# Attention units: the division by the softmax sums moved from VectorE into the turning product on TensorE

## The reference, cut to what matters

```
p = softmax(where(mask, sc, -inf), axis=-1)
attn = p[:, :, 0] - lam * p[:, :, 1]
outs.append(einsum("bhqk,bkhe->bqhe", attn, vb))
```

## Time and profile before

| what | value |
|---|---|
| median of three runs | 2226.13 us (2222.15 to 2226.5) |
| the profiled execution, its own time | 2225.26 us |
| its span, first to last instruction | 2223.5 us |
| its mean granted TensorE clock | 0.908 |
| units of the first attention | about 873 to 905 us |
| units of the two later attentions | about 1530 to 1563 and 1926 to 1960 us |

### The profile page before, as it was taken

The page is one execution under the profiler, slowest core; times in us unless marked ns, Lnnn a source line. Parts: engine busy times, 40 slices in busy tenths (PEclk is TensorE's granted clock), DMA queues, the critical chain, the costliest instruction groups (busy, mean ns, idle before and its releaser), DMA issues.

```text
span 2223.5 us, 33018 instructions
## 1 busy us (share of the span) xinstructions
PE 2064.7 (93%) x13605; PEld 1387.2 (62%) x13605; DVE 717.1 (32%) x2298; ACT 358.4 (16%) x968; POOL 86.6 (4%) x92
## 2 busy tenths in 40 slices
PE   8999999998889798899998989798999999899998
PEld 7687576665655544476665756444688644458863
DVE  4354242221222224532221222457322114732211
ACT  2122110100000012210000100114221001322100
POOL 0112100000000020000000000000001100000110
PEclk9999977998887999977887878899999999999999
DMA  9333359999999973369999999942244344224420
GB/s 344 128 108 115 142 203 398 425 425 424 424 425 425 406 255 113 129 259 426 424 424 424 424 425 423 377 157 76 97 154 155 131 160 165 76 86 152 152 95 19
DMA packets 112382, 565.33 MB, mean 254 GB/s; under 512 B 12456, under 2 KB 15726, under 8 KB 79470
## 3 DMA queue, kind: packets, MB, share of 16 engines
q1 hardware_dynamic: 112238, 563.21, 63.8%
HBM read 562.14 MB, written 1.05 MB: 253 GB/s over the span
## 4 chain that ended last, share of the span: by engine, by line
PE 86%; issue 4%; DVE 4%; DMA 4%; ACT 2%; SPq 1%; DVEq 0%; ACTq 0%
PE ps L2433 14%; PE ps L670 12%; PE ps L1634 11%; PE ps L651 10%; PE ps L296 9%; PE ps L709 7%; PE ps L1201 4%; DMA ring<-in_moe_w_up_dram 3%; PE ps L762 3%; PE ps L1307 3%; PE ps L1211 2%; PE ps L691 2%; PE ps L1975 1%; ACT arena L1771 1%; PE ps L1663 1%
## 5 line engine op out<-in xcount | busy, mean ns | idle before, releaser
L2433 PE MATMUL ps<-arena,ring 128*128 128x256 f32 (+1 forms) x1536 | 305.5, 362 | 0.0
L2433 PEld LDWEIGHTS ps<-arena,ring 128*128 128x128 f32 x1536 | 271.9, 190 | 33.9 <-issue 1.0
L651 PEld LDWEIGHTS ps<-arena 128*128 128x128 f32 x2048 | 251.5, 204 | 28.0 <-issue 27.0
L651 PE MATMUL ps<-arena 128*128 128x32 f32 x2048 | 258.4, 287 | 0.0
L1634 PE MATMUL ps<-ring,arena 128*128 128x512 f32 (+1 forms) x576 | 250.4, 594 | 3.3 <-DVE arena L421 3.3
L670 PE MATMUL ps<-ring,arena 128*32 128x256 f32 x2816 | 195.7, 435 | 41.0 <-issue 38.4
L296 PE MATMUL ps<-ring,arena 128*128 128x512 f32 x480 | 209.1, 596 | 0.8 <-ACT arena L2276 0.8
L1634 PEld LDWEIGHTS ps<-ring,arena 128*128 128x128 f32 x576 | 109.7, 192 | 135.4 <-issue 135.2
L670 PEld LDWEIGHTS ps<-ring,arena 128*32 128x32 f32 x2816 | 114.8, 126 | 121.1 <-issue 86.7
L296 PEld LDWEIGHTS ps<-ring,arena 128*128 128x128 f32 x480 | 91.4, 191 | 113.3 <-issue 111.9
L2493 DVE SCALAR_TENSOR_TENSOR arena<-ps,pcol,arena 128x255 f32<-128x255 f32 (+1 forms) x176 | 84.9, 482 | 210.8 <-ACT arena L2466 207.6
(11 more groups left out here) (305 smaller groups left out, 1904.1 us busy)
## 6 DMA issues: line engine op xcount, KB each, us to landing
ring<-in_moe_w_gate_dram SPq DMA_DIRECT2D x44, 2048.0 KB, 29.3
ring<-in_moe_w_up_dram SPq DMA_DIRECT2D x44, 2048.0 KB, 33.8
ring<-in_moe_w_down_dram SPq DMA_DIRECT2D x44, 2048.0 KB, 29.6
ring<-in_w_up_dram SPq DMA_DIRECT2D x22, 2048.0 KB, 8.0
arena<-in_moe_w_gate_dram SPq DMA_DIRECT2D x20, 2048.0 KB, 30.5
arena<-in_moe_w_up_dram SPq DMA_DIRECT2D x20, 2048.0 KB, 34.9
arena<-in_moe_w_down_dram SPq DMA_DIRECT2D x20, 2048.0 KB, 32.4
ring<-in_ssm_w_in_dram SPq DMA_DIRECT2D x12, 2048.0 KB, 10.2
```

The source lines that it names most:

```text
L651: mm = nc.tensor.matmul(ps[:, 4, k * CAP:(k + 1) * CAP], normed[:, tt, k, :], slots[:, b, tt, :], start=(tt == 0), stop=(tt == TT - 1))
L2433: mm = nc.tensor.matmul(ps[:, n % 4, lo:hi], w[:, k, k4 * P:(k4 + 1) * P], xT_mlp[:, k, lo:hi], start=(k == 0), stop=(k == KD - 1))
```

## The change

The probabilities stay unscaled. DVE writes two diagonal matrices for each unit, the identity times the reciprocal sum of each query row (in the first attention the second also times -lambda), and PE multiplies each 128 x 128 block of exponentials by the diagonal. The product comes out turned and scaled at once. In the first attention the blocks of c = 0 and c = 1 for the same keys are added in PSUM, which replaces `joined`. The diagonals lie in the place of `joined` in the first attention, and in a free area in the later ones. The exps, the mask, the copies out of PSUM and the values are as before. The diff, with the lines left out that only pass a flag on:

```diff
+        diag_first, diag_second = area(14336, 2, 2, P), area(22288, 2, 2, P)
...
         def pe_units(pe, units, pT, probs, joined):
+            inv_diag = diag_first if joined else diag_second
...
                 nk = u.kv // P
-                for c in range(1 if joined is not None else 2):
-                    src = joined[:, b, :] if joined is not None else probs[:, b, c, :]
-                    for kt in range(nk):
-                        at = (c * nk + kt) * P
-                        mm = nc.tensor.transpose(ps[:, 4 + b, at:at + P], src[:, kt * P:(kt + 1) * P], ident)
+                for kt in range(nk):
+                    for c in range(2):
+                        at = kt * P if joined else (c * nk + kt) * P
+                        mm = nc.tensor.matmul(ps[:, 4 + b, at:at + P], probs[:, b, c, kt * P:(kt + 1) * P],
+                                              inv_diag[:, b, c, :], start=(c == 0 or not joined),
+                                              stop=(c == 1 or not joined))
                 mm.then_inc(U["turned"].sem, 1)
...
                 V(nc.vector.reciprocal(st_inv[:, b, :], st_sum[:, b, :]))
-                if joined is not None:
-
-                    if n >= 2:
-                        dve.wait_ge(U["turned"].sem, U["turned"].at(n - 1))
-                    nc.vector.tensor_scalar(st_inv[:, b, 1:2], st_inv[:, b, 1:2], neg_lam, None, ALU.mult)
-                    V(nc.vector.tensor_scalar(joined[:, b, 0:u.kv], probs[:, b, 0, 0:u.kv], st_inv[:, b, 0:1], None,
-                                              ALU.mult))
-                    nc.vector.scalar_tensor_tensor(joined[:, b, 0:u.kv], probs[:, b, 1, 0:u.kv], st_inv[:, b, 1:2],
-                                                   joined[:, b, 0:u.kv], ALU.mult, ALU.add)\
-                        .then_inc(U["probs"].sem, 1)
-                else:
-                    nc.vector.tensor_tensor(probs[:, b, :, 0:u.kv], probs[:, b, :, 0:u.kv],
-                                            bcast(st_inv[:, b, :], u.kv), ALU.mult).then_inc(U["probs"].sem, 1)
+                if n >= 2:
+                    dve.wait_ge(U["turned"].sem, U["turned"].at(n - 1))
+                nc.vector.tensor_scalar(inv_diag[:, b, 0, :], ident, st_inv[:, b, 0:1], None, ALU.mult)
+                nc.vector.tensor_scalar(inv_diag[:, b, 1, :], ident, st_inv[:, b, 1:2], neg_lam if joined else None,
+                                        ALU.mult, *([ALU.mult] if joined else [])).then_inc(U["probs"].sem, 1)
```

More of the change, by code:

```diff
@@ L1740, in values @@
                 nk = u.kv // P
-                if joined is not None:
+                if joined:
                     for kt in range(nk):
@@ L1780, in copy_turned @@
                     act.wait_ge(U["out"].sem, U["out"].at(n - 1))
-                w = u.kv * (1 if joined is not None else 2)
+                w = u.kv * (1 if joined else 2)
                 nc.scalar.activation(pT[:, b, 0:w], ps[:, 4 + b, 0:w], ACT.Copy).then_inc(U["probsT"].sem, 1)
@@ L1855, in hybrid_stack @@
         probs = area(13312, 2, 2, SEQ)
-        joined = area(14336, 2, SEQ)
         pT = area(14848, 2, SEQ)
@@ L1963, in pe_attention1 @@
             pe.wait_ge(jobs_copied.sem, jobs_copied.at(8))
-            pe_units(pe, units, pT, probs, joined)
+            pe_units(pe, units, pT, probs, True)
             pe.wait_ge(U["copied"].sem, U["copied"].at(len(units)))
@@ L2017, in copy_out @@
                                             accum_out=ossq[:, u.i, u.pair:u.pair + 1])
-            act_units(act, units, sm, probs, pT, joined, copy_out)
+            act_units(act, units, sm, probs, pT, True, copy_out)
             head1.act_norm(act)
@@ L2055, in dve_attention1 @@
             dve_jobs(dve, head_jobs)
-            dve_units(dve, units, sm, probs, joined)
+            dve_units(dve, units, sm, probs, True)
             def scale_outputs(half):
@@ L2235, in pe_attention @@
                 pe.wait_ge(jobs_copied.sem, jobs_copied.at(15))
-                pe_units(pe, units, pT2, probs2, None)
+                pe_units(pe, units, pT2, probs2, False)
                 pe.wait_ge(U["copied"].sem, U["copied"].at(n_units))
@@ L2277, in copy_out @@
                                                 ACT.Copy)
-                act_units(act, units, sm2, probs2, pT2, None, copy_out)
+                act_units(act, units, sm2, probs2, pT2, False, copy_out)
                 for tt in range(TT):
@@ L2366, in dve_attention @@
                 dve_jobs(dve, head_jobs, 9)
-                dve_units(dve, units, sm2, probs2, None)
+                dve_units(dve, units, sm2, probs2, False)
                 def normalise(tt):
```

## The result

The changed kernel takes 2231.01 us (median of 11 runs, 2224.13 to 2237.49) against 2223.93 us for the kernel before in the same 11 rounds (2218.17 to 2228.47). The ratio is 1.0031 with a 95% interval of 1.0016 to 1.0045: 0.3% slower, as forecast in direction and in size (0.30%). The interval reaches from 3.6 to 10.0 us around a difference of 7.08. The profiled execution after has a span of 2232.8 us; its own time, 2234.59 us, is 3.6 above the median of its runs.

The account below looks back on a forecast made before the run. A loop of waits through the odd units, with no engine full, was taken to bound the unit stages. First attention 1.4, its lower-clock start 0.8, later attentions 4.6, clock -0.2: +6.6 us, 2232.7 us; range 2227.5 to 2237.5.

Parts of the forecast that it names:

- The forecast pairs: Time from odd turn to odd turn: 3.80 us in the first attention, 4.51 (dilated) and 3.69 (others) in the later ones.
- The price of a product: Turns on PE: a float32 product is two instructions, 0.11 us each further one, so an odd turn takes 1.16 us.
- a product costs four transposes: Rival for the turns on PE: sixteen steps an odd turn, +21 us over the sum, 2253 us; chance 0.03.
- The scaling of the identity: On DVE: costs nothing extra over scaling data, 0.28 us for 128 columns, 0.34 with two column operands.
- The tail of the first stage: End of the first attention: the chain goes from the last scaling to DVE's `scale_outputs`, so the eighth odd turn isn't counted.
- the start of the first attention: First turns at the lower clock, with PE on the chain: 0 to 1.3 us more than counted, taken as 0.8.
- the sum's seven turns and eight scalings: First attention: seven odd turns each 0.72 us longer, eight odd scalings each 0.46 us shorter, together +1.4 us.
- I wrote that it isn't full: PE in the first attention's pairs: busy 3.4 us of 3.80 after the change, so not full.
- a sign of being wrong: Among the conditions under which the prediction would be wrong: the even units come onto the chain.
- the clock pays back: Rival: busier PE keeps lower-clock windows away after and inside the later units; +2.9 to +4.6 us, around 2229.8; chance 0.17.
- the turn didn't hide: Rival for the turns on PE: added instructions cost nothing on the loop, total -6.0 us, 2220 us; chance 0.03.
- no lower window fell inside the later stages: Rival: lower clock within the units, six windows in the three stages, +5 us over the sum, 2237.5 us; chance 0.08.

Follow-up runs that it names:

- diag_unused: The changed kernel with diagonals written but unused, TensorE turning unscaled exponentials by plain transposes; first attention 30.29 us, later stages 32.34 and 32.49, whole run 12009.31 us.
- product_alone: The kernel before with each transpose replaced by an ordinary float32 product with the identity; first attention 34.56 us, later stages 38.01 and 38.45 us.
- after_halves: The changed kernel with an event for each diagonal, so the turn begins while the second is written; stages 33.55, 35.31 and 35.40 us.
- before_awake: The kernel before with six spare products on TensorE in the two waits ahead of the first attention's units; ratio 1.0023 (1.0009 to 1.0036).

## Why the prediction was right

**The loop and its parts.** It rested on one reading: that the loop through the odd units' scaling, turn, copy and exponentials sets the pace, so that every saving and every cost counts once an odd unit. diag_unused and product_alone took the two parts one at a time and gave -0.20 and +0.50 in the dilated kind, for forecasts of -0.21 and +0.50. The forecast pairs were 3.80, 4.51 and 3.69; measured 3.81, 4.52 and 3.75 (from ScalarE's copy to its next one). So the mechanism held, but that 6.6 us were forecast and 7.08 measured is closer than the noise allows to claim: the interval is 3.2 us to either side, and two terms below missed in opposite directions.

**The price of a product.** Two instructions at a step of 0.11 us, eight of them 1.16 us from idle: measured 1.16. The rival in which a product costs four transposes had 3 in 100. The Trainium skill, "TensorE: Matmul & The Clock Gate" (Terms), calls transpose mode four times faster for float32. Here the factor is two in instructions and 1.75 in time, 0.67 to 1.17 us for the same four blocks in product_alone, and the measurement decides.

**VectorE.** The scaling of the identity took 0.286 and 0.282, and up to 0.344 with two column operands, against 0.28 and 0.34 taken. The tail of the first stage went as forecast: it ends through DVE's `scale_outputs`, and that comes 1.08 us after ScalarE's last copy of turned blocks begins, against 1.80 before. So the last turn cost nothing, and the last saving counted.

**The term that was mis-sized: the start of the first attention.** I counted that turns cost twice there, bounded it by 0 and 1.3 us, and took 0.8. The stage is 3.20 us longer, and the sum's seven turns and eight scalings explain 1.4 of it; the rest, 1.8 us, is the start, beyond my upper bound. The first even turn takes 1.23 us instead of 0.48 and the first odd one 2.00 instead of 0.62. The even one before:

```profile
876.52 0.48 PE ps L1732
```

That is 2.1 us of added TensorE time. VectorE takes only some 0.3 off, ahead of the even turn: between the two turns TensorE is the chain, so its saving of 0.46 on the first odd unit, which the sum has among its eight, isn't gained there. The bound left that out.

**TensorE full in the plain kind.** I wrote that it isn't full, from the first attention alone. For plain pairs of the later layers it is: 3.75 instead of 3.69, after_halves gained nothing there but in the last pair, and the even turns stand on the chain (1564.62 above), which I had named as a sign of being wrong. The miss is small, since the loop and the engine's own work lie 0.06 apart. With it and the start and end of a stage, the later ones are 2.49 and 2.57 us longer at equal clock, for 2.3 forecast.

**The clock.** The windows at the lower level inside and behind the later stages are gone in the changed kernel; the MLP stretch is 358.0 instead of 359.9 us. Inside the third stage the window had cost 0.57 us (34.65 against 34.08), for which I had taken 0.2. That looks like the rival in which the clock pays back. The Trainium skill, "TensorE: Matmul & The Clock Gate" (Part 4), says that transposes don't count as busy in the same way, which would fit. But before_awake has the very units of before, with transposes, and lacks these windows too (358.4, and a third stage of 34.08). In before and in before_awake, 10 us that begin 0.2 and 1.3 us ahead of the output product (length, busy by engine, clock):

```profile
1563.50:1573.50 10.00, 9.78 (x19) 4.36 (x20) 0.69 (x1) 0.47 (x2) 0.00 (x0) 0.83 0.01 2
```

```profile
1568.00:1578.00 10.00, 9.38 (x29) 4.36 (x30) 0.69 (x1) 1.35 (x5) 0.00 (x0) 1.00 0.01 2
```

So the window can go while the units stay as they are, here in an execution whose stage began 5.5 us later, and I don't count its absence for the change. Of the four kernels with float32 products in the later units one (product_alone) has a lower window in a later stage or at its end, of the eight with transposes there five. Whether more work on TensorE makes such windows rarer stays open; single profiles don't settle it. The remaining rivals fell: the turn didn't hide (each added instruction cost its whole step), and no lower window fell inside the later stages after the change.

## What to carry to other kernels

A float32 transpose on TensorE is one instruction for 128 columns here and a float32 product is two, so folding a scaling into the turning product takes an odd turn from four instructions to eight, 0.67 to 1.16 us. It pays only where VectorE gives back more than that on the same loop, and here it gave back 0.21. With 16-bit exponentials and diagonals, less precise ones, the turn fell to 0.40 us and the same change paid. Before moving work to another engine, look for the wait in it: in the later layers two instructions with an event each in place of one that does both took 0.3 us off every odd unit and made the kernel 0.26% faster (halves), with the same instructions on TensorE and ScalarE and 32 more on VectorE. And measure an idle gap in a view of the whole engine before filling it.

## What the runs showed of the hardware that I had not expected

A ScalarE copy of 128 columns out of PSUM takes 0.368 us with a column as its scale and 0.277 without. A bfloat16 product of 128 columns has a step of 0.06 us against 0.11 for each of the two instructions of a float32 one, and four of them from idle take 0.40 us. The lower clock takes the step of a float32 instruction from 0.11 to 0.21 us, so it harms a turn in proportion to its instructions: eight products took 2.00 us instead of 1.16, two transposes 0.62 instead of 0.44. And ScalarE's idle time of 0.30 us a pair understated its room: a copy that begins behind one still running counts as no idle time, though it began 0.26 us after it instead of 0.16, and with the waits gone the pair was 0.45 us shorter (diag_unused).
